# A hybrid encoder in one kernel: the last tiles' normed rows moved from VectorE to GpSimd, and TensorE's work around the first prompt tile and the first expert reordered

## The reference

```python
for layer in range(DEPTH):
    h = rms_norm(x, norm_mix[layer])
    x = x + hybrid_mixer(h, ...)            # Fourier mixing + gated recurrence, then @ w_out
    h = rms_norm(x, norm_ffn[layer])
    x = x + expert_choice_ffn(h, w_router, w_gate, w_up, w_down)
return rms_norm(x, norm_final)

def expert_choice_ffn(h, ...):              # 16 experts, each picks its tokens
    affinity = softmax(xt @ w_router)
    g, idx = top_k(affinity.T, cap)         # cap: 128 of the sample, 64 of the prompt
    xe = xt[idx]
    he = silu(xe @ w_gate) * (xe @ w_up)
    ye = (he @ w_down) * g
    out = zeros_like(xt).at[idx].add(ye)
```

## Time and profile before

| | us |
|---|---|
| median of 3 runs | 2576.37 (2573.74 to 2576.71) |
| the profiled execution's own time | 2574.17 |
| its span, first to last instruction | 2572.4 |
| TensorE busy | 2524.8 (98%) |
| VectorE busy | 1644.0 (64%) |
| ScalarE busy | 1330.6 (52%) |
| GpSimd busy | 322.9 (13%) |
| mean granted clock of TensorE | 0.995 of full speed |

### The profile page before, as it was taken

One profiled execution on the slowest core, in us unless ns is written; L12 is line 12 of the kernel. 1 busy time (PEld: TensorE's weight loads), 2 busy tenths in 40 slices (PEclk: granted clock), 3 DMA queues, 4 the chain that ended last, 5 costly groups with the idle time before them and its releaser, 6 DMA issues.

```text
span 2572.4 us, 45120 instructions
## 1 busy us (share of the span) xinstructions
PE 2524.8 (98%) x18541; PEld 2276.5 (88%) x18541; DVE 1644.0 (64%) x1929; ACT 1330.6 (52%) x1546; POOL 322.9 (13%) x241
## 2 busy tenths in 40 slices
PE   8999999999998999999999999999999999999998
PEld 6777777788876999999999999999999999999997
DVE  6555555435387666767666676766767666676767
ACT  6434353424544555555555555555555555555556
POOL 3102020101102010120202102020120202102010
PEclk9999999999998999999999999999999999999999
DMA  4101010136436676776767667676676767667677
GB/s 158 30 18 55 2 55 2 61 118 213 170 131 234 226 259 232 250 247 235 251 228 253 240 237 257 224 256 233 247 246 235 250 228 254 239 241 253 228 254 282
DMA packets 64135, 503.67 MB, mean 196 GB/s; under 512 B 7552, under 2 KB 7936, under 8 KB 39712
## 3 DMA queue, kind: packets, MB, share of 16 engines
q1 hardware_dynamic: 47872, 448.82, 48.2%
q0 software_dynamic: 16160, 53.38, 7.1%
HBM read 465.00 MB, written 37.22 MB: 195 GB/s over the span
## 4 chain that ended last, share of the span: by engine, by line
PE 66%; DVE 2%; ACT 1%; issue 0%; POOL 0%; DVEq 0%; ACTq 0%
PE up_banks_b L2214 15%; PE up_banks_a L2214 15%; PE up_banks_b L2217 6%; PE up_banks_a L2217 6%; PE up_banks_b L2255 2%; PE up_banks_b L2253 2%; PE up_banks_b L2254 2%; PE up_banks_b L2252 2%; PE up_banks_a L2256 2%; PE up_banks_b L2256 2%; PE up_banks_a L2255 2%; PE up_banks_a L2253 2%; PE up_banks_a L2252 2%; PE up_banks_a L2254 2%; PE up_banks_b L2212 1%; PE up_banks_a L2212 1%
## 5 line engine op out<-in xcount | busy, mean ns | idle before, releaser
L1983 DVE TENSOR_TENSOR big_lo<-wide,big_hi 128x4096 fp32r<-128x4096 f32 x189 | 836.4, 4425 | 418.9 <-ACT big_hi L1749 418.8
L1749 ACT CAST big_hi<-wide 128x4096 fp32r<-128x4096 f32 x190 | 689.8, 3630 | 522.8 <-PE up_banks_a L2214 240.9
L2214 PE MATMUL up_banks_b<-x_parts,big_hi 128*128 128x384 f32 x2016 | 574.3, 356 | 0.0
L2214 PE MATMUL up_banks_a<-x_parts,big_hi 128*128 128x384 f32 x1984 | 565.0, 356 | 1.0 <-DVE h_parts L2007 1.0
L2217 PE MATMUL up_banks_b<-x_parts,big_lo 128*128 128x192 f32 x1764 | 442.0, 251 | 0.0
L2217 PE MATMUL up_banks_a<-x_parts,big_lo 128*128 128x192 f32 x1736 | 435.0, 251 | 0.0
L2214 PEld LDWEIGHTS up_banks_b<-x_parts,big_hi 128*128 128x128 f32 x2016 | 365.3, 189 | 0.2
L2214 PEld LDWEIGHTS up_banks_a<-x_parts,big_hi 128*128 128x128 f32 x1984 | 359.4, 189 | 1.9 <-DVE h_parts L2007 1.2
L2217 PEld LDWEIGHTS up_banks_b<-x_parts,big_lo 128*128 128x128 f32 x1764 | 336.1, 191 | 0.0
L2217 PEld LDWEIGHTS up_banks_a<-x_parts,big_lo 128*128 128x128 f32 x1736 | 330.8, 191 | 0.6
L65 PE MATMUL bank<-big_hi,w_hi 128*128 128x512 f32 x576 | 236.8, 411 | 0.0
(11 more groups left out here) (349 smaller groups left out, 4166.7 us busy)
## 6 DMA issues: line engine op xcount, KB each, us to landing
wide<-in_expert_weights SPq DMA_DIRECT2D x190, 2048.0 KB, 7.7
w_raw<-in_w_heads SPq DMA_DIRECT2D x48, 256.0 KB, 2.8
x_in<-in_x SPq DMA_DIRECT2D x12, 512.0 KB, 4.2
x_d<-in_x POOLq DMA_DIRECT2D x12, 512.0 KB, 4.3
residual<-x_d POOLq DMA_DIRECT2D x12, 512.0 KB, 2.9
ffn_in<-h_and_xT_d POOLq DMA_DIRECT2D x12, 512.0 KB, 3.3
wide<-residual SPq DMA_DIRECT2D x12, 512.0 KB, 6.4
tab<-in_tables POOLq DMA_DIRECT2D x10, 512.0 KB, 7.1
```

The costliest lines, as they stand in the source:

```text
L1749: nc.scalar.copy(ahead.hi(c), raw[:, c % RAW]).then_inc(hi_done, 1)
L1983: nc.vector.tensor_tensor(ahead.lo(c), raw[:, c % RAW], ahead.hi(c).bitcast(F32), ALU.subtract).then_inc(lo_done, 1)
L2214: last = nc.tensor.matmul(out[:, 0:2 * CAP], hi, x[:, k], start=n == 0, stop=n == KT - 1, skip_group_check=True)
```

## The change

- GpSimd makes the normed rows of tiles 7 to 11, with two multiplies in place of the fused instruction, after it has stored the tile's sum (and, for tile 11, after the gather is issued). It waits for all constants once before its loop.
- GpSimd makes the second half of chunk 0's low parts at t = 10 of its loop; VectorE makes the first half at t = 6.
- At t = 7 ScalarE rounds the first two prompt pieces ahead of the root, VectorE makes their low parts right behind their sums, and TensorE multiplies the EARLY pieces of both halves ahead of turning the affinities.
- The additions of tile 11 stand behind tile 10's negated maximum rather than behind its affinities.
- TensorE makes six idle transposes ahead of the chosen tokens' transposes, and 16 rather than 8 at the beginning of block 3.
- In block 3 `sample_high(1)` stands ahead of the wait for the prompt lists.

```diff
 WEIGHTS_HIGH = {5: (0, slice(0, 4), False), 6: (0, slice(4, KT), True), 9: (1, slice(0, 4), False), 10: (1, slice(4, KT), True)}
-WEIGHTS_LOW = {6: slice(0, 4), 7: slice(4, KT)}
+POOL_NORM = S_TILES - 1
 LATE_HEADS = {1: (4, 5), 2: (6, 7), 3: (8, 9), 4: (10, 11)}
...
 x2_stored, h_stored = stored
+scaled = sem("rows_scaled")
 squared, rooted, inverted, h_ready = sem("x2_squared"), sem("x2_rooted"), sem("x2_inverted"), sem("h2_ready")
...
         pool.wait_ge(wo_lo_done, KT)
+        pool.wait_ge(const_loaded, 64)
+
+        def normed(s):
+            pool.wait_ge(inverted, s + 1)
+            pool.wait_ge(h_stored, 16 * s)
+            nc.gpsimd.tensor_tensor(h, x[:, s % 2], stat[:, RSTD, s:s + 1].to_broadcast([P, D]), ALU.mult)\
+                .then_inc(scaled, 1)
+            pool.wait_ge(scaled, s - POOL_NORM + 1)
+            nc.gpsimd.tensor_tensor(h, h, nf[:], ALU.mult).then_inc(h_ready, 1)
+
         for t in range(TT + 1):
...
                 pool.dma_start(x[:, t % 2], x_dram[row:row + P]).then_inc(x_loaded[t % 2], 16)
+            if t == S_TILES + 2:
+                for k in range(4, KT, 2):
+                    made = ahead.low_early(pool, nc.gpsimd, 0, slice(k, k + 2))
+                made.then_inc(ahead.lo_done, 1)
             if t >= 1:
...
                         .then_inc(ahead.gathered, 16)
+                if s >= POOL_NORM:
+                    normed(s)
                 pool.wait_ge(h_ready, s + 1)
...
                 turned(t)
+            if t == S_TILES - 1:
+                prompt_high((0, 1))
             act.wait_ge(squared, t + 1)
...
             if t == S_TILES - 1:
-                prompt_high((0, 1))
                 prompt_read((2, 3))
...
                     dve.sem_inc(ahead.chosen, 1)
-        for t in range(TT):
-            head_low(LATE_HEADS.get(t, ()))
+        def add_rows(t):
             dve.wait_ge(x_loaded[t % 2], 16 * (t // 2 + 1))
...
                     .then_inc(added, 1)
+
+        for t in range(TT):
+            head_low(LATE_HEADS.get(t, ()))
+            if t < TT - 1:
+                add_rows(t)
             if t == S_TILES - 1:
                 prompt_sums((0, 1))
+                for g in (0, 1):
+                    low_of(g, 0, 2 * GROUPS + g + 1, ob[g][:])
             sample_rounds(PAUSES[t][0])
...
             dve.wait_ge(added, 2 * t + 2)
-            nc.vector.scalar_tensor_tensor(out=h, in0=x[:, t % 2], scalar=stat[:, RSTD, t:t + 1], in1=nf[:],
-                                           op0=ALU.mult, op1=ALU.mult).then_inc(h_ready, 1)
+            if t < POOL_NORM:
+                nc.vector.scalar_tensor_tensor(out=h, in0=x[:, t % 2], scalar=stat[:, RSTD, t:t + 1], in1=nf[:],
+                                               op0=ALU.mult, op1=ALU.mult).then_inc(h_ready, 1)
             if t == S_TILES - 1:
-                for g in (0, 1):
-                    low_of(g, 0, 2 * GROUPS + g + 1, ob[g][:])
                 prompt_sums((2, 3))
-            if t in WEIGHTS_LOW and t < S_TILES - 1:
-                ahead.low_early(dve, nc.vector, 0, WEIGHTS_LOW[t])
+            if t == S_TILES - 2:
+                ahead.low_early(dve, nc.vector, 0, slice(0, 4))
             sample_rounds(PAUSES[t][1])
...
                                     ALU.mult, ALU.mult).then_inc(negmax, 1)
+            if t == TT - 2:
+                add_rows(TT - 1)
             sample_rounds(PAUSES[t][2])
...
             dve.wait_ge(sum_inv, t + 1)
-            if t in WEIGHTS_LOW and t == S_TILES - 1:
-                ahead.low_early(dve, nc.vector, 0, WEIGHTS_LOW[t]).then_inc(ahead.lo_done, 1)
             first, _, row = LISTS[list_of(t)]
...
                 product(t + 1, 0, EARLY)
+                product(t + 1, 1, EARLY)
                 turn_affinities(1)
                 product(t + 1, 0, LATE)
-                product(t + 1, 1, K_ORDER)
+                product(t + 1, 1, LATE)
                 continue
...
             route(t)
+        for _ in range(6):
+            nc.tensor.transpose(banks[1][:, 0:P], ident[:], ident[:])
         pe.wait_ge(ahead.chosen, 1)
...
                 nc.tensor.transpose(set_b[:, 3, 0:P], ident[:], ident[:])
-        keep_running(8)
+        keep_running(16)
         pe.wait_ge(gathered, 16)
...
         sample_low(0)
+        sample_high(1)
         pe.wait_ge(chosen, 2)
...
             nc.tensor.transpose(s_bank[0][:, i * ROWS:(i + 1) * ROWS], lists, ident[0:ROWS, 0:ROWS]).then_inc(back, 1)
-        sample_high(1)
         pe.wait_ge(hi_done, BY_TOKENS)
```

## The result

The changed kernel took 2581.05 us in the median of 20 runs, the kernel before 2575.53 on the same chip, 5.5 us less. The ratio, which is worked out from all executions but one of the kernel before that took 7409.55 us, is 1.0026 [1.002, 1.0033], about 6.7 us **slower** where I had forecast 2.9 faster, and the median is outside my range. The profiled execution took 2579.9 us, its span is 2578.1.

What follows compares the result with a forecast made beforehand. TensorE, busy 98%, bounds the kernel. Of 6.1 us won at tile 7, 3.45 remain after the store and 0.7 at block 3; with warming and reordering, 2.9 us off 2576.37 gives 2573.5, range 2568.5 to 2577.5.

Steps and rivals of the forecast that it cites:

- Part 1: First prompt tile (t=7): both TensorE waits and the slow matmuls go, so tile 10's routing starts 6.1 us earlier.
- Part 2: Tile 11's additions follow tile 10's negated maximum; TensorE turns the rows from 765.1 instead of 772.95.
- Part 3, the passes: Normed rows on GpSimd: 2.4 us a pass, 4.9 for a tile's two with a semaphore between them.
- a sign of being wrong: GpSimd's passes for the normed rows: off the assumed 2.4 us by more than 0.3.
- Part 3, the store: Tile 10's store lands in 5.0 us; ScalarE's square of tile 11 begins at 769.1 instead of 773.52.
- the other sign: Store of normed rows that the square waits for: landing beyond 6 us would show the prediction wrong.
- the store is not disturbed: Tile 10's store lands in 3.2 us despite the weight load; 4.8 us gained, 2571.6; chance 0.22.
- Part 4: Block 3's start: sixteen warming transposes take 3.25 us; the first product starts at 788.4 instead of 788.05.
- Part 5: First expert's new order: the 3.02 us wait and slow matmuls vanish; prompt rows' transposes start 2.9 us earlier in all.
- My losing one: GpSimd's passes of tiles 10 and 11 slowed by VectorE to 4.18 us each: 2581.9; chance 0.09.
- at the block's end VectorE idles: Argument against GpSimd's passes being slowed by VectorE: VectorE idles beside tile 11's passes at the block's end.

Runs made afterwards that it cites:

- e3: Changed kernel, with chunk 2's weight load waiting for tile 10's store and chunk 3's for all row stores; 2569.08 us, ratio 0.9978.
- e2: Changed kernel, with only chunk 3's weight load waiting until all stores of normed rows have landed; 2574.60 us, ratio 0.9998.
- e6: Kernel before, with only the first expert's new order (second chunk's products ahead of the prompt lists' wait); 2571.90 us, ratio 0.9987.
- e10b: Changed kernel with both load waits, without the six idle transposes and with 8 instead of 16 at block 3; 2566.58 us, ratio 0.9966.
- e7: Changed kernel with tiles 10 and 11's rows on VectorE, no six idle transposes, 8 instead of 16 at block 3; 2565.61 us, ratio 0.9963.

## Why the prediction was wrong

**Part 1: right.** Tile 10 is routed 5.93 us earlier (6.1 forecast), in every kernel with the new order of tile 7 within 0.02 us.

**Part 2: right.** Tile 11's rows are turned 7.75 us earlier (7.85).

**Part 3, the passes: the second right, the first priced too high.** 1.89 and 2.40 us for 2.4 each, from the first one's start to the second one's end 4.36 (4.9). The multiply by one value a row is cheaper than a pass over two full operands, which I had no row for. The first pass is off by 0.51 us, more than the 0.3 that I had named as a sign of being wrong, but to the kernel's good.

**Part 3, the store: the step that failed first.** "Landing takes 2.9 to 5.1 us for these stores and up to 6.6 for a residual store; [...] I take 5.0". I had seen the load come "into the same moment" and took about the longest landing of these stores before, 5.1, which was that of tile 11's store beside the gather. The 6.6 us store went out 3.5 us behind its load, when part of it had landed; none of these stores in the trace of before went out 0.6 us behind one. A landing beyond 6 was the other sign that I had named. Tile 10's took 8.9 us, the square began at 62.96 instead of the forecast 59.05, and 3.87 us were lost at tile 11's routing. 2.56 are left at block 3's beginning, since the stretch from the transposes back to there takes 7.53 us and not 9.1: the passes took 0.54 less, the gather's issue 1.03 instead of 1.45, and the block's end does not wait for the 0.6 us of the store's issue (GpSimd's second pass ended at 783.72, TensorE began at 784.53); the routing and the six transposes took 0.26 more than I had priced. The rival "the store is not disturbed" had the better size of the prize: 4.8 us (4.7 by its own terms, as 763.7 + 3.2 + 0.4 is 767.3 and not 767.1); e3, which makes it so for both stores, has 6.12 at the prompt rows.

**Part 4: an omission, and the costlier one.** I priced the sixteen transposes (3.25; measured 3.44) and let the first product follow them. I did not ask who waits for the store of tile 11, which the change had put at the very end of the block. ScalarE's first copy does, and SP issues chunk 3's load at the block's beginning, 0.19 us behind the store. In the kernel before that store went out at 779.73, right behind the gather's issue and 3.9 us ahead of chunk 3's load (783.65), and landed after 5.1 us, 0.9 ahead of ScalarE's first copy (785.77). Nobody waited for it, so no row showed the wait. That is 4.55 us at the first product beyond what was already late (7.30 less 2.75); e2 takes 4.29 of it away, the rest is a stretch that I had priced a little short.

**Part 5: right in itself, undone by part 4.** "The 3.02 us wait and the slow matmuls behind it vanish": in e6 they do, 3.45 us. But in the changed kernel TensorE came cold from its 4.32 us wait, and the products that stand ahead of the lists' transposes took 11.57 us instead of 9.2. VectorE's last row for the lists:

```profile
803.49 0.22 DVE L997 COPY table<-wide 16x128 f32<-16x128 f32 x1
```

They were ready at 803.71 and turned at 806.64: the new order, which was to hide a wait, made the gather wait 2.9 us for TensorE.

The sum at the prompt rows, measured less forecast: 2.56 to block 3's beginning, 0.19 for the transposes, 4.55 for the second store, 2.37 for the cold products, less 0.42 behind them: 9.25. And -2.90 + 9.25 = 6.35, the row in the table.

**The rivals.** My losing one had the right engine, GpSimd, and the right sign, and the wrong mechanism: its passes were to be slowed, and they were not. That its 2581.9 lies near the measured 2581.05 is luck. What I had against it, "at the block's end VectorE idles", was wrong as well (below), but it cost little. The range missed since I had bounded the unknown landing by rows of other distances, and left the second store out of the question.

## What to carry to other kernels

When a change moves a store, look up what else is issued within a few microseconds of its new place, and everyone who waits for its landing, also those who never had to wait so far: a wait that always came free leaves no row in the profile. A transfer that somebody waits for is best kept out of the shadow of a large load; where it can't be earlier, a wait of the load on the store costs less than the collision, as long as the load has slack. And work that is to keep an engine running is only worth its place where the engine has nothing to do anyway.

## What was new about the hardware

A 512 KB store issued 0.64 us behind or 0.19 ahead of a 2 MB load took 8.9 and 9.0 us, against 2.9 to 3.0 without it; 1.05 us ahead of it, 3.1 and 3.2. Half of tile 10's delay is the sharing, packet by packet; half is the late first packet, 4.0 us after the issue instead of 1.0.

VectorE waits for GpSimd in one kind of instruction. The last affinity is a multiplication of 128x16 values. The timeline of DVE of the changed kernel:

```profile
778.74 2.59 DVE L1390 TENSOR_SCALAR affinity<-ex_d,stat_d 128x16 f32<-128x16 f32 x1
```

It ends at 781.33, and GpSimd's first pass, above, at 781.29; when it began, GpSimd was issuing the gather (778.33 to 779.36), so here it stood still from before the pass on, and whether the gather's issue held it as well isn't shown. In e10b, DVE's and then POOL's row:

```profile
773.76 1.40 DVE L1391 TENSOR_SCALAR affinity<-ex_d,stat_d 128x16 f32<-128x16 f32 x1
...
773.21 1.91 POOL L1157 TENSOR_TENSOR h_and_xT_d<-x_d,stat_d 128x1024 f32<-128x1024 f32 x1
```

Here it begins inside the pass and ends with it, at 775.16 and 775.12. In e7, with no pass beside it, DVE has:

```profile
776.99 0.23 DVE L1390 TENSOR_SCALAR affinity<-ex_d,stat_d 128x16 f32<-128x16 f32 x1
```

The changed kernel has it at tile 7 too, where the affinity takes 1.56 us and ends at 719.28, with GpSimd's second pass (719.26) and only 0.22 us before TensorE turns it: a little more would have brought part of the old wait back. The rounds' instructions beside the passes were not slowed. The Trainium skill (SBUF — State Buffer, Who interferes with whom) states it so: VectorE's instructions with two inputs in SBUF and its 2-port modes, which a multiplication by a value can enter, wait for the whole of a GpSimd instruction that began first. The rows of e10b agree, 1.17 us lost on a 0.23 us instruction; in the changed kernel it is 2.36. Little of it counted at the block's end, as GpSimd's second pass ended the block 0.11 us behind VectorE anyway.
